# Dense groups one place earlier in the attention steps of a fused two-part layer kernel

## The reference

```python
proj = h @ w_in
qa, ka, va, qb, kb, vb, qc, kc, vc, fz = jnp.split(proj, cuts, axis=-1)
oa = diff_attention(rope(qa), rope(ka), va, lam)       # 4 heads, two maps each, causal; then a norm by head
ob = dilated_mixture_attention(rope(qb), rope(kb), vb) # 6 heads, dilated causal patterns
oc = forgetting_attention(qc, kc, vc, cum_logf)        # 6 heads, causal, with a forget term on the scores
o = jnp.concatenate([merge(oa), merge(ob), merge(oc)], axis=-1)
return o @ w_out
```

## Time and profile before

| | us |
|---|---|
| median of 3 runs | 3120.99 (3120.82 to 3121.11) |
| the profiled execution | 3119.96 |
| its span, first to last instruction | 3118.2 |
| PE busy | 2886.8 (93%) |
| DVE busy | 1637.1 (53%) |
| ACT busy | 1113.8 (36%) |
| mean granted clock of PE | 0.947 |
| attention steps, layer one | 1703 to 1965 |
| attention steps, layer two | 2436 to 2699 |

### The profile page before, as it was taken

One profiled execution on the slowest core, in us unless ns is written; L12 is line 12 of the kernel. 1 busy time (PEld: TensorE's weight loads), 2 busy tenths in 40 slices (PEclk: granted clock), 3 DMA queues, 4 the chain that ended last, 5 costly groups with the idle time before them and its releaser, 6 DMA issues. The chain is left out here.

```text
span 3118.2 us, 37948 instructions
## 1 busy us (share of the span) xinstructions
PE 2886.8 (93%) x14756; PEld 2357.1 (76%) x14756; DVE 1637.1 (53%) x2921; ACT 1113.8 (36%) x1712; POOL 162.9 (5%) x160
## 2 busy tenths in 40 slices
PE   6988899999798899999987998899997998899998
PEld 5777788887686777888866877788886787778886
DVE  5736566655664557555665544553544543464442
ACT  6434322224353433222344344332322444332231
POOL 1200000002121000000020000000000000000000
PEclk9987899999898889999988999999998999999999
DMA  4110144443221013444403111222322210122322
GB/s 151 68 41 28 41 176 175 150 152 111 90 84 41 28 41 132 154 160 162 162 34 128 62 35 35 68 86 97 108 73 92 68 53 19 65 89 76 113 78 78
DMA packets 43282, 281.06 MB, mean 90 GB/s; under 512 B 6105, under 2 KB 6361, under 8 KB 11737
## 3 DMA queue, kind: packets, MB, share of 16 engines
q1 hardware_dynamic: 43096, 278.54, 25.7%
HBM read 276.42 MB, written 2.10 MB: 89 GB/s over the span
## 5 line engine op out<-in xcount | busy, mean ns | idle before, releaser
L304 DVE TENSOR_TENSOR low_panels<-raw_panels,high_panels 128x2048 fp32r<-128x2048 f32 (+3 forms) x218 | 469.3, 2153 | 325.9 <-ACT high_panels L292 325.8
L292 ACT ACTIVATE high_panels<-raw_panels 128x2048 fp32r<-128x2048 f32 (+3 forms) x218 | 392.5, 1801 | 475.3 <-PE bank L1492 152.0
L421 PE MATMUL bank<-mlp_h_high,high_panels 128*128 128x512 f32 x1152 | 457.1, 397 | 0.0
L421 PE MATMUL bank<-mlp_h_low,high_panels 128*128 128x512 f32 x1152 | 455.2, 395 | 0.0
L421 PE MATMUL bank<-mlp_h_high,low_panels 128*128 128x512 f32 x1152 | 455.0, 395 | 0.0
L421 PEld LDWEIGHTS bank<-mlp_h_high,low_panels 128*128 128x128 f32 x1152 | 215.9, 187 | 52.8
L421 PEld LDWEIGHTS bank<-mlp_h_high,high_panels 128*128 128x128 f32 x1152 | 216.0, 188 | 52.0
L421 PEld LDWEIGHTS bank<-mlp_h_low,high_panels 128*128 128x128 f32 x1152 | 216.0, 188 | 51.6
L446 PE MATMUL bank<-high_panels,h_high 128*128 128x256 f32 x704 | 213.1, 303 | 8.4 <-DVE arena L1179 7.8
L421 PE MATMUL bank<-h_high,high_panels 128*128 128x512 f32 x496 | 207.2, 418 | 0.2
L1492 PE MATMUL bank<-mlp_hid_high,high_panels 128*128 128x512 f32 x512 | 204.3, 399 | 0.0
(11 more groups left out here) (349 smaller groups left out, 5068.5 us busy)
## 6 DMA issues: line engine op xcount, KB each, us to landing
raw_panels<-in_w SPq DMA_DIRECT2D x238, 1024.0 KB, 4.9
raw_panels<-in_w SPq DMA_DIRECT2D x16, 384.0 KB, 3.2
raw_panels<-in_w SPq DMA_DIRECT2D x4, 960.0 KB, 4.7
raw_panels<-in_w SPq DMA_DIRECT2D x4, 768.0 KB, 4.3
row<-in_row SPq DMA_DIRECT2D x2, 1220.0 KB
x<-in_xT SPq DMA_DIRECT2D x2, 1024.0 KB, 6.1
raw_panels<-in_w SPq DMA_DIRECT2D x4, 512.0 KB, 3.5
mix<-in_rope SPq DMA_DIRECT2D x2, 1024.0 KB, 8.3
```

What stands on the lines that cost most here:

```text
L292: self.nc.scalar.activation(self.g.high[:, i % SPLIT, 0:raw.shape[1]], raw, ACT.Copy).then_inc(self.high_ready, 1)
L304: self.nc.vector.tensor_tensor(self.g.low[:, i % SPLIT, 0:w], raw, self.g.high[:, i % SPLIT, 0:w].bitcast(F32), ALU.subtract).then_inc(sel ...
L421: ins = nc.tensor.matmul(bank[:, :], w[a][:, k, c0:c0 + P], rhs[b][:, k0 + k, :], start=first and k == 0 and j == 0, stop=last and k == kt ...
```

## The change

In the step loops of PE and of ACT the dense groups of step i go from the end of the step to its head. DVE's loop, `dense_at` and everything else stay.

```diff
@@ PE @@
                 for i in range(n_steps):
+                    for j in dense_at.get(i, []):
+                        dense(j)
                     if i < n_pairs:
                         scores(i)
                     if 2 <= i < n_pairs + 2:
...
                         turn(i - 1)
                     if i in chunks_at:
                         turn_chunk(chunks_at[i])
-                    for j in dense_at.get(i, []):
-                        dense(j)
                 for i in second_groups:
                     dense(i)
@@ ACT @@
                 for i in range(n_steps):
+                    for j in dense_at.get(i, []):
+                        evict(j)
                     if i < n_pairs:
                         softmax(i)
                     if 1 <= i < n_pairs + 1:
...
                     if i in chunks_at:
                         chunk(chunks_at[i])
-                    for j in dense_at.get(i, []):
-                        evict(j)
                 for i in second_groups:
                     evict(i)
```

## The result

The changed kernel takes 3125.39 us (median of 20 runs, 3121.37 to 3130.35) against 3120.59 (20 runs, 3112.13 to 3124.80) for the kernel before: ratio 1.0018, interval 1.0011 to 1.0025, so 5.6 us slower (3.4 to 7.8): the loss is clear of the noise, though it is less than the 0.2% that counts as a change. The profiled execution took 3121.45 us, span 3119.6; it is the second fastest of the 20, so it may show less loss than a typical one. Single executions differ by up to 12.7 us with the kernel before and 9.0 with the changed one, far more than the three runs of before had shown; the mean granted clock of the changed kernel's runs lies between 0.943 and 0.948. A microsecond can therefore only be read from medians of many runs, or from the gaps of the profile, which hardly vary.

What follows compares the result with a forecast made beforehand. PE, busy 93% of the span, was taken as the bound, so only its idle or slow time counts. Idle time +1.8 and clock -1.7 gave +0.1 us on the median: 3121.1 us, 8-in-10 range 3115.5 to 3126.5.

Steps and rivals of the forecast that it cites:

- The change seen as a shift by one step: PE and ACT loops: each dense group comes one step earlier, the cycle stays the same, DVE keeps its place.
- C: Bare transitions (no dense group) at steps 17, 21, 25 after the change: PE gaps of 0.05 and 0.78, 0.83 us.
- D: Bare transitions at steps 19, 23, 27 after the change: PE gaps of 0.54 and 0.57, 1.11 us.
- A: Bare transitions at steps 18, 22, 26 before the change: PE gaps of 0.53 and 0.47, 1.00 us; no clock falls.
- B: Long bare transitions at steps 20, 24, 28 before the change: PE gaps of 0.57 and 1.54, 2.11 us.
- Idle time: PE in both layers' attention: +0.1-1.4+2.2 = +0.9 us a layer, +1.8 in both, bounds +1.0 and +4.
- The wait at 33: First output group at step 33: PE idles about 2.75 us a layer for DVE's low part of the last chunk.
- The swap's wait: Step 6, behind a value group: PE waits for DVE's multiplication of the previous swap, charged 0.1 us a layer.
- the third rival: Steps 3 and 5: late panel data delays DVE, PE stands in the swap; +6.4 us, 3127.5 us, chance 0.08.
- The clock: PE's falls to half clock in attention: four instead of five, -1.7 us, bounds -8.0 and +1.7.
- Rival 4: Clock falls come of something other than these gaps and stay five; +1.8 us alone, 3122.8 us, chance 0.10.
- rival 1: The clock falls at all six sites, long transitions and step-33 waits; +3.5 us, 3124.5 us, chance 0.17.

Runs made afterwards that it cites:

- e3: The kernel before with only the first output group, of step 33, moved to the head of its step; +11.2 us against before.
- e1: The changed kernel with only the first output group put back at the end of step 33; -5.0 us against the kernel before.
- e2: The kernel before with only the groups of steps 0 to 26 at the head of their steps; -2.2 us against before.
- g1: The kernel before with one exchange on PE alone, turn(i-1) ahead of result(i-2) in each step; -19.7 us against before.
- f1: The changed kernel, but an output group waits for each chunk's low part just ahead of that chunk's matmuls; -2.8 us against the kernel before.
- h1: The kernel before with only the groups of steps 0 to 24 at the head, so step 27 stays covered; -4.4 us against before.
- g4: The changed kernel with turn(i-1) put ahead of result(i-2) on PE; -15.9 us against the kernel before.

## Why the prediction was right or wrong, point by point

- **The change seen as a shift by one step** held: the changed profile has C and D gaps where A and B stood, no gaps at steps 35 and 39, and at 34 and 38 gaps of 0.52 and 0.29, and 0.53 and 0.30 us (forecast 0.53 and 0.29). C was forecast 0.05+0.78 and is 0.07+0.80, D was 0.54+0.57 and is 0.55+0.58. The rule read from one transition gave the others.
- **Idle time**, forecast +1.8, is +2.2, inside its bounds. The wait at 33 was sized 2.75 and is 2.4 and 2.8; it is shorter in layer one because PE came to it at half clock (1906.3 to 1909.7), and so later. The swap's wait, charged at 0.1, is 0.38, and the result at step 8 waits 0.15 where I had expected none: 0.3 to 0.4 us a layer short. Nothing of the third rival (swaps at steps 3 and 5 late by a late panel) showed: PE waited in one swap of each layer, at step 6.
- **The clock** is the step that failed. The forecast was one fall fewer, -1.7 us, by three saved at the B sites and two added at 33. The two were added, in both layers of the change's profile and of e3's, at about 1.5 us each; the three mostly weren't saved, for e1 and e2 gain about their idle time (half clock -1.2 +-2.0 and -0.8 +-3.0 us). The failed step is "takes away four B sites, with three of the falls, leaves four with two": I took the chance of a fall as belonging to a site, and the remaining sites took the falls over. In the six kernels with the shift steps 28 and 32 fell 21 times of 24, where I had counted two of four, and the short transitions of kind C, which I took as safe, had a fall in 5 of 12 layers. So the sign "a clock of 1.00 in steps 16 to 27" held in layer two and not in layer one (0.97, a fall at step 17). Idle time +2.2 and two falls, +3.1, give +5.3; measured is +5.6. What moves the falls is open.
- **Rival 4**, falls that don't come of these gaps, is wrong for step 33 and half right for the rest, as their number hardly fell with two of the four long transitions. The profiled execution of the change shows five falls, as that of before, and stands 3.9 us under the median: one profile isn't enough to count them, and the forecast number of four rested on one. The Trainium skill's rule, cited in the prediction (TensorE: Matmul & The Clock Gate, section "Why this matters for your kernels"), would leave the clock untouched by waits as short as these. The runs disagree: group 33 ran at a mean clock of 0.67 behind waits of 2.4 and 2.8 us, and at 1.00 in before and e1, which have no such wait.
- **The direction**: +0.1 was forecast with 0.80 on no change. The measured 0.18% is at the slow edge of that, inside the stated range, and nearest to rival 1. The interval, 3.4 to 7.8, leaves out +0.1: of the 5.5 us between, 0.4 are idle time and about 5 the clock. That it still lies in the range is the range's width, and not the count of falls.

## What to carry to other kernels

Write the order of a software pipeline out over several steps before costing it: moving a block from the end of a step to its head changes nothing of the cycle, only which neighbours the block covers and which inputs it meets before they are ready. Read the price of each bare transition as one chain (here turn, pass, exp, keep) against the work between its ends; where the gap follows that rule, the next edit is to put independent work inside the chain, which was worth 19.7 us here (g1), where the question asked was one of 5.6. A block whose inputs come in pieces should wait piece by piece (f1). And the falls of the clock shouldn't be priced site by site from one profile: cover one site, and count them again over several.

## What wasn't expected of the hardware

- The same program differs by 13 us from execution to execution (3112.13 to 3124.80 for the kernel before). Much of it lies outside the attention steps: over the fourteen profiles the rest of the kernel, which the edits leave alone, spent between 298 and 320 us at half clock. The changed kernel's executions go with their mean granted clock (0.948 for 3121.4 us, 0.943 for 3130.4). Three runs that agreed within 0.3 us did not show it.
- A clock fall at step 28 came in 3 of 8 layers with the long transitions at 20 and 24 bare, and in 13 of 14 where they were covered. Covering the step ahead of it took the fall away in neither layer (h1).
- Waits of 2.2 to 2.8 us ahead of a group were followed by half clock in four of four layers (the change and e3), and so were g4's, of 2.3 and 1.7 us, though PE was at half clock already ahead of the second; transitions that idle 2.1 us in two pieces, in some only.
